# Layer 0 of a two-layer step: layer 1's first eight modulation units read in the last attention tile, and the first expert weights split among the norms

## What is computed

```python
shift1, scale1, gate1, shift2, scale2, gate2 = split(silu(c) @ w_ada[l] + b_ada[l], 6)
h = rms_norm(x, norm1) * (1 + scale1) + shift1
q, k, v, su, sv, cb, cc, cx = split(h @ w_in)
merged = concat(rms_norm(attention), rms_norm(sgu), rms_norm(conv))
x = x + gate1 * (merged @ w_out)
h2 = rms_norm(x, norm2) * (1 + scale2) + shift2
x = x + gate2 * moe(h2)        # top-1 of 4 groups, top-2 of its 4 experts
```

## Time and profile before

| | us |
|---|---|
| median of 3 runs | 1110.79 (1108.39 to 1112.57) |
| the profiled execution | 1111.54 |
| its span, first to last instruction | 1109.7 |
| TensorE busy / VectorE / ScalarE / GpSimd | 987.5 / 668.7 / 587.1 / 247.5 |
| mean granted TensorE clock | 0.951 |

### The profile page before, as it was taken

How to read it: one execution, slowest core, us unless ns; L and a number is a source line. 1 busy time by engine, 2 the same in 40 slices (tenths; PEclk the granted TensorE clock), 3 DMA queues, 4 the chain that set the end, 5 groups by cost and what they waited for, 6 DMA issues and landing times.

```text
span 1109.7 us, 15792 instructions
## 1 busy us (share of the span) xinstructions
PE 987.5 (89%) x5588; PEld 759.7 (68%) x5588; DVE 668.7 (60%) x970; ACT 587.1 (53%) x929; POOL 247.5 (22%) x304
## 2 busy tenths in 40 slices
PE   4899989986998699998989999899789739999984
PEld 2688865765874588887757887467568637888861
DVE  0359125655276799988444831455625659999936
ACT  4452235655222598887267222565623418988822
POOL 3034015211131122230411500620203212222031
PEclk9899999999998799999999999899889959999998
DMA  9695227553156899996771321565313448999944
GB/s 319 235 276 205 76 62 273 194 183 130 34 214 249 333 387 401 417 401 260 297 209 40 111 79 39 200 242 200 115 57 133 150 167 329 408 417 411 366 154 173
DMA packets 89091, 248.16 MB, mean 224 GB/s; under 512 B 25773, under 2 KB 30381, under 8 KB 79817
## 3 DMA queue, kind: packets, MB, share of 16 engines
q1 hardware_dynamic: 75960, 209.54, 50.9%
q0 software_dynamic: 11632, 32.60, 8.5%
q10 hardware_dynamic: 1440, 5.24, 1.2%
HBM read 220.82 MB, written 30.21 MB: 226 GB/s over the span
## 4 chain that ended last, share of the span: by engine, by line
PE 68%; DVE 9%; DMA 9%; ACT 7%; issue 4%; SPq 1%; POOL 0%; ACTq 0%; DVEq 0%; POOLq 0%
PE ps L1559 12%; PE ps L1561 12%; PE ps L1560 12%; DMA pool<-in_moe_w 6%; PE ps L1566 4%; PE ps L1568 4%; PE ps L1567 4%; PE ps L1577 4%; PE ps L1749 3%; PE ps L1764 3%; PE ps L1959 2%; PE ps L1738 2%; DVE wL L1358 2%; ACT wH L938 2%; PE ps L1898 2%
## 5 line engine op out<-in xcount | busy, mean ns | idle before, releaser
L1559 PE MATMUL ps<-wH,actH 128*128 128x512 f32 x608 | 248.6, 409 | 10.0 <-DVE actL L1487 5.2
L1561 PE MATMUL ps<-wH,actL 128*128 128x512 f32 x608 | 240.9, 396 | 0.0
L1560 PE MATMUL ps<-wL,actH 128*128 128x512 f32 x608 | 240.1, 395 | 0.0
L1358 DVE TENSOR_TENSOR wL<-raw,wH 128x2048 fp32r<-128x2048 f32 x64 | 146.2, 2285 | 14.1 <-ACT wH L938 13.6
L1559 PEld LDWEIGHTS ps<-wH,actH 128*128 128x128 f32 x608 | 116.5, 192 | 38.4 <-issue 9.1
L1561 PEld LDWEIGHTS ps<-wH,actL 128*128 128x128 f32 x608 | 116.0, 191 | 26.0
L1560 PEld LDWEIGHTS ps<-wL,actH 128*128 128x128 f32 x608 | 116.7, 192 | 22.2
L938 ACT ACTIVATE wH<-raw 128x2048 fp32r<-128x2048 f32 x64 | 122.3, 1911 | 16.4 <-DMA raw<-in_moe_w 16.2
L1566 PE MATMUL ps<-wH,actH 128*128 128x512 f32 x256 | 105.2, 411 | 5.4 <-DVE wL L1358 2.8
L1568 PE MATMUL ps<-wH,actL 128*128 128x512 f32 x256 | 102.0, 398 | 0.0
L1567 PE MATMUL ps<-wL,actH 128*128 128x512 f32 x256 | 101.3, 396 | 0.0
(11 more groups left out here) (261 smaller groups left out, 1662.6 us busy)
## 6 DMA issues: line engine op xcount, KB each, us to landing
raw<-in_moe_w SPq DMA_DIRECT2D x96, 512.0 KB, 8.6
raw<-in_w_ada SPq DMA_DIRECT2D x40, 1024.0 KB, 5.0
raw<-in_moe_w SPq DMA_DIRECT2D x16, 1024.0 KB, 12.6
pool<-in_moe_w SPq DMA_DIRECT2D x32, 512.0 KB, 7.8
pool<-in_moe_w SPq DMA_DIRECT2D x16, 1024.0 KB, 11.4
ys<-pool SPq DMA_DIRECT2D x32, 512.0 KB, 11.0
raw<-in_w_in SPq DMA_DIRECT2D x15, 1024.0 KB, 8.7
raw<-in_w_ada SPq DMA_DIRECT2D x16, 512.0 KB, 11.5
```

Source lines behind the costliest of these rows:

```text
L1358: dve.tensor_tensor(wL[:, w, :], mraw[parity][i], f32(wH[:, w, :]), ALU.subtract).then_inc(sem(f"m_lo{i}"), 1)
L1559: pe.matmul(out, aH, wH[:, slot_, cols_], start=first, stop=False)
L1560: pe.matmul(out, aH, wL[:, slot_, cols_], start=False, stop=False)
L1561: return pe.matmul(out, aL, wH[:, slot_, cols_], start=False, stop=last)
```

## The change

The order of STREAM: w_out's four units no longer come in a row, but layer 1's eight units come between them as three, three and two. Layer 0's quarters of unit 9 start one step later (`gap`), after u = 35 instead of at it. TensorE reads one of the eight units in each of the steps u = 33 to 40 (NEXT_AT), all sums in bank 7; `piece_add` stands at u = 41 on VectorE, and `merged_chunk(1)`, the first to use bank 7 again, waits for it. `bias_in` for them stands behind the issue of the scale rows on POOL. All `ada_next` calls go. The two first `m_split`s stand where layer 1 has them, on both engines. The semaphore `first_gathers` and SP's wait for `m_g0` go.

Cut to its core:

```diff
@@ -55,9 +55,9 @@
 for _l in range(DEPTH):
-    STREAM += [("w", _l, n) for n in range(int(_l == 0), 8)] + [("ada", _l, n) for n in range(8, 24)] + [("w", _l, n) for n in range(8, 12)]
-    if _l + 1 < DEPTH:
-        STREAM += [("ada", _l + 1, n) for n in range(8)]
+    STREAM += [("w", _l, n) for n in range(int(_l == 0), 8)] + [("ada", _l, n) for n in range(8, 24)]
+    NEXT = [("ada", _l + 1, n) for n in range(8 if _l + 1 < DEPTH else 0)]
+    STREAM += [("w", _l, 8)] + NEXT[0:3] + [("w", _l, 9)] + NEXT[3:6] + [("w", _l, 10)] + NEXT[6:8] + [("w", _l, 11)]
     START.append(len(STREAM))
@@ -257,13 +257,9 @@
-        QUARTER_AT = {31 + i: (8 + i // 4, i % 4) for i in range(8)}
-        def ada_bank(l, q):
-            return 6 if l and q == 0 else 7
+        QUARTER_AT = [{31 + i + (gap if i >= 4 else 0): (8 + i // 4, i % 4) for i in range(8)} for gap in (1, 0)]
+        NEXT_AT = {NLT * NH + 1 + i: i for i in range(KD)}
@@ -471,9 +467,6 @@ SP
                 sp.wait_ge(sem("h2"), at("h2", l, NT))
-                if l == 0:
-                    sp.wait_ge(sem("m_g0"), 16)
                 load_w13(1, 1, None, 1)
@@ -610,6 +603,8 @@ POOL, after the scale2 rows (and taken out behind the shift2 rows)
+                if l + 1 < DEPTH:
+                    bias_in(l + 1, 0)
                 rest_stats(3)
@@ -951,26 +942,20 @@ ScalarE, among the norms
                 h2_store(3)
-                if l + 1 == DEPTH:
-                    w_read(act, l, 9)
-                    m_split(0, 0, pairs)
+                w_read(act, l, 9)
+                m_split(0, 0, pairs)
...
-                if l + 1 == DEPTH:
-                    w_read(act, l, 10)
-                    m_split(1, 0, pairs)
+                w_read(act, l, 10)
+                m_split(1, 0, pairs)
                 h2_store(4)
                 lT_out(4)
                 w_read(act, l, 11)
-                if l + 1 < DEPTH:
-                    m_split(0, 0, pairs)
-                    m_split(1, 0, pairs)
@@ -1305,6 +1290,8 @@ VectorE, attention
                     if u in HALF_AT:
                         half_add(l, HALF_AT[u])
+                    if l + 1 < DEPTH and u == NT * NH + 1:
+                        piece_add(l + 1, 0)
@@ -1367,9 +1354,8 @@ VectorE, norms
                 normalised(4)
-                if l + 1 == DEPTH:
-                    m_split(0, 0, first)
-                    m_split(1, 0, first)
+                m_split(0, 0, first)
+                m_split(1, 0, first)
@@ -1463,13 +1449,6 @@ VectorE, after the lists
-                if l + 1 < DEPTH:
-                    dve.wait_ge(sem("first_gathers"), at("first_gathers", l, 1))
-                    m_split(0, 0, first)
-                    piece_add(l + 1, 0)
-                    m_split(1, 0, first)
@@ -1780,6 +1759,10 @@ TensorE, attention, behind the ada units of ADA_AT
+                    if l + 1 < DEPTH and u in NEXT_AT:
+                        if NEXT_AT[u] == 0:
+                            pe.wait_ge(sem("piece_done"), at("piece_done", l, 3))
+                        ada_mm(l + 1, NEXT_AT[u])
@@ -1789,6 +1772,8 @@ TensorE, merged_chunk
+                        if t == 0 and k == 1 and l + 1 < DEPTH:
+                            pe.wait_ge(sem("piece_done"), at("piece_done", l + 1, 1))
@@ -1839,7 +1819,6 @@ TensorE, and so for (2, 3), (3, 4), (4, 5) and (5, KD) further down
-                ada_next(0, 2)
```

More of the change, by code:

```diff
@@ L84 @@
     "x_half": NT, "x_attn": NT, "ss2": 2 * NT, "rstd2": NT, "h2": NT, "h2T_psum": NT, "h2T": NT, "h2_stored0": 48, "h2_stored1": 32, "logits": NT, "lT_psum": NT, "lT": NT,
-    "rt_exp_in": 2, "rt_exp": 2, "choice": 1, "counts_psum": 1, "lists": 1, "list_psum": 1, "idx_ready": 1, "first_gathers": 1, "ctl_ready": 1, "gates": 2,
+    "rt_exp_in": 2, "rt_exp": 2, "choice": 1, "counts_psum": 1, "lists": 1, "list_psum": 1, "idx_ready": 1, "ctl_ready": 1, "gates": 2,
     "diags": 2 * NT, "y_sum": NT, "moe_split_done": 1, "x_moe": NT,
@@ L626, in _ @@
                     pl.dma_start(frow, row(I["final_norm"])).then_inc(sem("final_row"), 16)
-                if l + 1 < DEPTH:
-                    bias_in(l + 1, 0)
                 for t in range(NT):
@@ L659, in _ @@
                     pl.sem_inc(sem("m_idx"), 1)
-                pl.sem_inc(sem("first_gathers"), 1)
                 pl.wait_ge(sem("ctl_ready"), at("ctl_ready", l, 1))
@@ L881, in _ @@
                             accum_out=rsum[:, u % 16:u % 16 + 1]).then_inc(sem("prob"), 1)
-                    if u in QUARTER_AT:
-                        quarter_hi(*QUARTER_AT[u])
+                    if u in QUARTER_AT[l]:
+                        quarter_hi(*QUARTER_AT[l][u])
                     if u == NLT * NH + 5:
@@ L1078, in piece_add @@
                     dve.wait_ge(sem("piece_out"), at("piece_out", l, 0))
-                dve.tensor_tensor(piece[q], ps[:, ada_bank(l, q), :], bpiece[q], ALU.add).then_inc(sem("piece_done"), 1)
+                dve.tensor_tensor(piece[q], ps[:, 7, :], bpiece[q], ALU.add).then_inc(sem("piece_done"), 1)
             def half_add(l, i):
@@ L1086, in half_add @@
                     dve.wait_ge(sem("bias_in"), bias_count(l, q))
-                    dve.tensor_tensor(piece[q], ps[:, ada_bank(l, q), :], bpiece[q], ALU.add).then_inc(sem("piece_half"), 1)
+                    dve.tensor_tensor(piece[q], ps[:, 7, :], bpiece[q], ALU.add).then_inc(sem("piece_half"), 1)
                 else:
                     dve.wait_ge(sem("piece_half"), at("piece_half", l, q))
-                    dve.tensor_tensor(piece[q], ps[:, ada_bank(l, q), :], piece[q], ALU.add).then_inc(sem("piece_done"), 1)
+                    dve.tensor_tensor(piece[q], ps[:, 7, :], piece[q], ALU.add).then_inc(sem("piece_done"), 1)
             def modc_out(l):
@@ L1294, in _ @@
                         pair_out((u - 5) // 2)
-                    if u in QUARTER_AT:
-                        quarter_lo(*QUARTER_AT[u])
+                    if u in QUARTER_AT[l]:
+                        quarter_lo(*QUARTER_AT[l][u])
                     if u >= 16 and u % 8 == 0:
@@ L1576, in ada_mm @@
                 for j in range(4):
-                    m = pe.matmul(ps[32 * j:32 * j + 32, ada_bank(l, q), :], c32, raw[:, POS["ada", l, n] % RAWS, j * N:(j + 1) * N],
+                    m = pe.matmul(ps[32 * j:32 * j + 32, 7, :], c32, raw[:, POS["ada", l, n] % RAWS, j * N:(j + 1) * N],
                                   start=(kt % group == 0), stop=(kt % group == group - 1))
@@ L1799, in _ @@
                 merged_chunk(1)
[L1801 to L1804, removed]
                 def h2_chunks(t):
@@ L1863, in _ @@
                 router_sum(1)
-                ada_next(2, 3)
                 router(2)
@@ L1867, in _ @@
                 router_sum(2)
-                ada_next(3, 4)
                 h2_chunks(4)
                 router(3)
-                ada_next(4, 5)
                 router(4)
@@ L1883, in _ @@
                 m.then_inc(sem("counts_psum"), 1)
-                ada_next(5, KD)
                 pe.wait_ge(sem("lists"), at("lists", l, 1))
```

## The result

| | median (runs) | profiled run | its span | granted clock |
|---|---|---|---|---|
| before | 1109.59 us (1108.26 to 1112.57) | 1111.54 | 1109.7 | 0.951 |
| after | 1128.06 us (1126.08 to 1131.46) | 1131.46 | 1128.7 | 0.940 |

The change makes the kernel slower: ratio 1.0175, 95% interval [1.015, 1.020]. By the medians that is +18.5 us, where +18.7 was forecast (1129.5 against the 1110.79 that was known then; the median of before has one run more here). The profiled execution of after is the slowest of its four, 3.4 above their median, so the profiles differ by 19.9.

A forecast was written before the change was run, and what follows sets the result against it. TensorE was taken to hold 68% of the chain, DMA and VectorE 9% each. 1111.54 + 19.0 (attention) - 0.3 (output projection to experts) + 0 (experts) = 1130.2, less 0.75 for the median: 1129.5 us, 8-in-10 range 1121 to 1136.

The forecast's parts named there:

- The ring of raw buffers: Layer 0's last attention tile: w_out units w8, w9, w10 share buffer 0; ada unit a6 queues behind w10; attention +19.0 us.
- The price of a load: Loads of w_out and ada units: 5.1 us for one finding the queues empty, 7.7 for the second of a burst.
- w9's last quarter: Layer 0's last attention tile: the last quarter of w_out's second unit is done at 270.6 instead of 263.35, +7.3 us.
- Behind a6: From a6's landing at 278.3 to the first output-projection matmul at 294.5, partly at low clock; attention +19.0 us in all.
- From the output projection to the first expert matmul: Layer 0 after attention, modelled on layer 1: -2.3 + 4.0 - 2.0 = -0.3 us, bounds -4.3 to +1.7.
- S1: First output-projection matmul to the fifth second-half product: 62.57 us instead of 64.90, 2.3 less.
- S3: Router sum to the first expert matmul: 19.63 us instead of 21.61, 2.0 less.
- S2: Fifth second-half product to the router sum: 13.75 us instead of 9.73, 4.0 more, with expert splits among the norms.
- Layer 1 unchanged: All of layer 1: its length was forecast to stay the same.
- B: Rival: the stall is there but later stages give more back (1123.5), or the clock stays up (1126.6); chance 0.14.
- C: Rival: slower still, with low clock in u = 36 to 38, loads at 6.6 us and collisions, 1135.5; chance 0.11.
- D: Rival: loads come in time, attention loses only 1.4 us, -4.3 and -2 behind it, 1106; chance 0.05.

The follow-up runs named there:

- w10_last: The changed kernel with w_out's unit w10 put behind a7, the last ada unit, in the load order, buffers unchanged: 1116.95 us, ratio to before 1.0068.
- warm_wait: The changed kernel with 84 dummy transposes of the identity on TensorE ahead of a6's matmuls: 1127.44 us (one run).
- five_not_loaded: The changed kernel without the loads of a3 to a7, TensorE multiplying what the buffers hold: 1115.13 us (one run).
- ring_free: The changed kernel with w9 two units earlier, w10 behind the ada units, no gap step, units read at other steps: 1112.46 us, ratio to before 1.0032.
- splits_late: The changed kernel with layer 0's two first expert splits back behind the norms and router, as before the change: 1124.64 us, ratio to before 1.0126.
- before_warm: The kernel before with dummy transposes of the identity (12, 12 and 28) in three idle TensorE stretches of both layers: 1100.82 us, ratio to before 0.9906.
- ring_free_late: ring_free with layer 0's two first expert splits late, as in splits_late: 1106.76 us, ratio to before 0.9975.

## Why the prediction was right, point by point

**The ring of raw buffers**: right. SP issues w9 at 251.84 (251.7 said) and w10 at 272.31, 0.02 us behind w9's last quarter on VectorE (271.60 + 0.69 = 272.29). w10_last shows the cause.

**The price of a load**: right. w9 was issued at 251.84 and ScalarE took it at 256.85: 5.0, forecast 5.1. w10's issue to a6's first matmul is 280.08 - 272.31 = 7.8, forecast 7.7. The 4.4 us as an estimate for one unit from the Trainium skill ("DMA: Bandwidth & Descriptors", section Anatomy of one DMA) is too low here too; the trace doesn't agree with it. (Worked out by that figure, the second load of a burst lands after 4.4 + 2.4 = 6.8 us instead of 7.7, so the two waits would be 1.8 shorter, not the 1.6 that I wrote.)

**w9's last quarter** was mis-sized. 270.6 was forecast and it came at 272.29; of the 1.7, 0.14 is that this execution is that much later at w8. a3 was read at 259.34 as forecast, but the step gave it 1.0 us, and it took 1.94: the clock was at 0.50 behind the 4.07 us pause:

```profile
259.34:261.28 1.94, 1.94 (x9) 0.28 (x9) 0.00 (x0) 0.00 (x0) 0.15 (x1) 0.50 0.98 410
```

I had the cold price in hand and used it for a6 alone. That is 0.9 of the 1.7. The scores of u = 37 behind it were still slow (1.34 from their start to that of the transposes, where 0.9 was forecast), another 0.4. From there to the end of the scores of u = 39 it took the 6.4 us forecast. The last 0.4 is the ring at the end: 3.3 from the row maximum at 269.00 to 272.29 and not 2.90, as ScalarE made a copy (269.57, 0.70 us) ahead of the exponential. The term is +8.8 where it was put at +7.3.

**Behind a6** the error went the other way. From a6's matmuls to the output projection 294.5 - 278.3 = 16.2 was forecast, and 294.81 - 280.08 = 14.7 measured, both by the chain's mark. a6 itself was at the low clock (1.93), but the transposes took 1.33 and the value product 1.31, 2.6 together where 3.6 stood, and a7 1.06 where 1.3 stood: TensorE was back at the full clock after some 3 us of work, while I had carried layer 1's 2.40 for a value product over to here. So 1.8 late (280.08 against 278.3) and 1.5 early nearly cancel, and 294.5 against the chain's 294.81 is closer than the reasoning deserves: that part is luck. +19.0 forecast, 294.81 - 275.52 = +19.3 measured. By the same error the price of the low clock behind a6's wait was put too high: 19.0 - 16.1 = 2.9 in the prediction, 1.4 in warm_wait.

**The smaller edits**: right. `piece_add` runs at 286.76 for 0.68, in the shade of the last pairs; `bias_in` is issued at 247.05 and followed by 9.43 us in which POOL is idle (10.87 in the earlier trace rows).

**From the output projection to the first expert matmul** -0.3 was forecast and +1.7 came (97.94 against 96.24 by the chain's marks), the upper bound. S1 by the chain's marks was 63.20 (62.57 forecast), S3 19.68 (19.63). S1 is 0.6 of the miss, and the larger term that failed is S2: 15.06, not 13.75. Layer 1 was the right model for the mechanism but its 13.75 was one draw: in after layer 1 itself shows 903.18 - 888.69 = 14.49, and layer 0 in w10_last 13.73. The other profiles with early splits come near the forecast of the whole stretch: by timeline marks it is 96.58 in before and w10_last, 96.61 in warm_wait, 96.74 in five_not_loaded and 96.14 in ring_free, and 98.29 in after. So +1.7 is the profiled execution of after, not the change. The router's transposes and matmuls, TensorE after the pause:

```profile
359.54 0.30 PE L1805 MATMUL ps<-gsel,pool 128*128 128x20 f32 x2
362.66 1.08 PE L1799 MATMUL ps<-pool,rw 128*32 128x128 f32 x16 [2.83 <-ACT pool L920]
363.68 1.97 PE L1791 MATMUL ps<-ident,pool 128*128 128x128 f32 x8
365.72 1.95 PE L1791 MATMUL ps<-ident,pool 128*128 128x128 f32 x8
```

The splits' own part, 4.0, was in the sum; splits_late (9.60 without them) and w10_last (13.73 with them) bear it out. The 1.3 on top came with the low clock.

**Experts**: 157.09 against 158.02: -0.9, within the 2 allowed.

**Layer 1 unchanged**: this one fell, in the profiled execution at least. Its stretch up to its output projection is 5.2 shorter than in before's, what follows 4.2 longer. The ten experiments' profiles have 273.9 to 278.0 for the stretch where before has 281.8, and before_warm, with the order of loads of before but with dummies, has 275.3. So the change of load order isn't needed for the shorter time. Of the 5.2, about 2.3 lie in layer 1's first attention tile, where the clock was 0.77 in before and 0.89 in after (windows, before and then after):

```profile
700.00:715.00 15.00, 13.90 (x81) 6.46 (x81) 7.22 (x19) 6.83 (x25) 14.66 (x5) 0.77 0.75 275
...
716.00:731.00 15.00, 13.39 (x89) 7.07 (x88) 7.95 (x20) 7.86 (x28) 14.61 (x6) 0.89 0.63 228
```

What sets the clock there in one execution and not in another stays open, as only one execution of before is profiled. It also means that part of the 8.3 us of before_warm (6.6 in this stretch by the profiles) may be such a draw and not the dummies; its timed ratio doesn't hang on the one profile, but its split by stages does. Its attention stage is 1.5 longer than before's, for instance: a value product ran at the low clock there (266.77, 2.37 us) ahead of all dummies.

**The rivals.** B needed the splits to hide, and they cost 4 to 5.5; or the clock to stay up, and it fell. Of C's 3 us more in attention only a3's 0.9 and the 0.4 behind it came. D's condition, that w10 and a6 land in time, is what ring_free makes true: attention then grows by 3.7 (2.3 in ring_free_late), where D had 1.4, the 6.3 us that D takes off behind it don't come, and the kernel still isn't faster than before. D was wrong about its own size as well as its condition.

## What to carry to other kernels

When loads are interleaved in one queue over a ring of few buffers, write down for each load whose last use frees its buffer: a load with a free buffer waits behind one without, and here moving that one issue by two places took 11 of the 18.5 us back. Work put between norms to fill an engine lengthens the path of every step that waits for that engine, and if TensorE then pauses, it may pay a second time through its clock. Price the matmuls after any wait at both clocks, and write the difference into the range: here the same pause was followed by the one in some executions and by the other in others. Last, two errors of nearly equal size hid each other here; only the steps show it, not the total.

## What the runs showed of the hardware

The clock fell in more places than I had expected. It was down after the 4.07 us pause (an ada unit at 1.94 instead of 1.06), after the 2.83 us pause in after's router stage (eight transposes at 1.97), and in ring_free at 259.32 in a tile with no wait for a load. It came back soon: in after the value product 3.1 us behind the pause of 10.44 ran at its usual 1.31. The Trainium skill ("TensorE: Matmul & The Clock Gate", Part 1) says that an idle TensorE is throttled to 1.2 GHz until it has been busy again; the traces agree for the pauses of 4.07, 4.16 and 10.44 us. For shorter ones they show that the same pause in the same place is followed now by the one clock, now by the other: behind 2.83 us in the router stage eight transposes took 1.97 in after and 1.09 in w10_last and warm_wait; behind 1.09 and 0.98 us in the last tile an ada unit took 1.93 in ring_free and 1.07 in ring_free_late. What decides between the two no run here shows.

Idle TensorE time that was filled with 104 useless transposes made the kernel before 8.3 us faster (ratio 0.9906 [0.9876, 0.9937]), over twice what the best order of the ada units gave (3.5). In all three kernels with them both output projections start at a granted clock of 1.00, where without them it is 0.50 to 0.74 in the first 5 us; layer 0's experts start at 0.50 to 0.66 with them all the same, two pauses after the dummies.
